# Second feed-forward stage: gate and up as seven block products of operand sums, in two passes of 544 tokens

## What is computed

```python
def swiglu(h, w_gu, w_down):
    gate, up = jnp.split(h @ w_gu, 2, axis=-1)
    return (jax.nn.silu(gate) * up) @ w_down
x = x + 0.5 * gt3 * swiglu(modulate(x, norm_ffn2, sh3, sc3), ffn2_w_gu, ffn2_w_down)
```

## Time and profile before

| | us |
|---|---|
| runs | 2447.24, 2447.64, 2450.85 |
| median of the runs | 2447.64 |
| span of the profiled execution | 2446.0 |
| PE busy in it | 2352.2 |
| DVE / POOL / ACT busy | 1107.6 / 537.6 / 386.4 |

### The profile page before, as it was taken

One profiled execution on the slowest core, in us unless ns is written; L12 is line 12 of the kernel. 1 busy time (PEld: TensorE's weight loads), 2 busy tenths in 40 slices (PEclk: granted clock), 3 DMA queues, 4 the chain that ended last, 5 costly groups with the idle time before them and its releaser, 6 DMA issues. The chain is left out here.

```text
span 2446.0 us, 50603 instructions
## 1 busy us (share of the span) xinstructions
PE 2352.2 (96%) x21666; PEld 2240.6 (92%) x21666; DVE 1107.6 (45%) x2446; ACT 386.4 (16%) x890; POOL 537.6 (22%) x278
## 2 busy tenths in 40 slices
PE   6999999999999989999888898999999999999997
PEld 5899999999999989888568885999999999999997
DVE  3634443334444365434676665147333444433344
ACT  4100000000000142434621123140000000000003
POOL 2412112212121032101331124313211212122111
PEclk8999999999999999999999999999999999999999
DMA  9232231110111042000310002332111011111102
GB/s 340 78 108 73 86 103 52 34 51 26 43 51 52 26 125 70 27 27 27 134 43 4 5 8 71 106 104 69 52 35 51 17 51 51 51 51 34 51 9 74
DMA packets 160634, 151.22 MB, mean 62 GB/s; under 512 B 21488, under 2 KB 141985, under 8 KB 160088
## 3 DMA queue, kind: packets, MB, share of 16 engines
q1 hardware_dynamic: 159960, 146.75, 19.2%
q10 hardware_dynamic: 144, 2.23, 0.2%
q0 software_dynamic: 384, 0.07, 0.0%
HBM read 137.98 MB, written 11.34 MB: 61 GB/s over the span
## 5 line engine op out<-in xcount | busy, mean ns | idle before, releaser
L487 PE MATMUL bank<-hh,f_up_hi 128*128 128x368 f32 (+1 forms) x2064 | 676.8, 328 | 1.9 <-POOL hl L412 1.0
L489 PE MATMUL bank<-hh,f_up_lo 128*128 128x368 f32 (+1 forms) x2064 | 674.7, 327 | 0.0
L488 PE MATMUL bank<-hl,f_up_hi 128*128 128x368 f32 (+1 forms) x2064 | 674.0, 327 | 0.0
L1224 DVE TENSOR_TENSOR f_prod<-f_silu,bank 128x368 f32<-128x368 f32 x132 | 70.3, 532 | 766.4 <-PE bank L489 760.1
L502 DVE SCALAR_TENSOR_TENSOR x<-bank,mods,x 128x368 f32<-128x368 f32 (+1 forms) x544 | 306.3, 573 | 200.4 <-PE bank L489 187.5
L487 PEld LDWEIGHTS bank<-hh,f_up_hi 128*128 128x128 f32 x2064 | 387.3, 188 | 7.4 <-issue 7.3
L488 PEld LDWEIGHTS bank<-hl,f_up_hi 128*128 128x128 f32 x2064 | 387.4, 188 | 0.0
L489 PEld LDWEIGHTS bank<-hh,f_up_lo 128*128 128x128 f32 x2064 | 387.4, 188 | 0.0
L955 POOL TENSOR_TENSOR f_up_lo<-f_up_raw,f_up_hi 128x2048 fp32r<-128x2048 f32 x44 | 203.3, 4621 | 776.8 <-DVE f_up_hi L1211 776.8
L487 PE MATMUL bank<-f_a_hi,f_dn_hi 128*128 128x368 f32 (+1 forms) x1056 | 346.6, 328 | 0.8 <-DVE f_scratch L505 0.8
L489 PE MATMUL bank<-f_a_hi,f_dn_lo 128*128 128x368 f32 (+1 forms) x1056 | 345.3, 327 | 0.0
(11 more groups left out here) (383 smaller groups left out, 2883.2 us busy)
## 6 DMA issues: line engine op xcount, KB each, us to landing
f_up_raw<-in_ffn_w_gu SPq DMA_DIRECT2D x88, 512.0 KB, 5.0
f_dn_raw<-in_ffn_w_down SPq DMA_DIRECT2D x22, 1024.0 KB, 7.5
ada<-in_w_ada SPq DMA_DIRECT2D x12, 1024.0 KB, 16.2
late<-in_w_ada SPq DMA_DIRECT2D x12, 1024.0 KB, 5.0
w_in_raw<-in_w_in SPq DMA_DIRECT2D x16, 512.0 KB
gates<-in_w_ada SPq DMA_DIRECT2D x8, 1024.0 KB, 5.8
x_in<-in_x_prompt SPq DMA_DIRECT2D x8, 512.0 KB, 8.5
gate<-in_w_ada SPq DMA_DIRECT2D x4, 1024.0 KB, 4.9
```

The source lines that it names most:

```text
L487: pe.matmul(out, wh, rh, start=(n == 0), stop=False)
L488: pe.matmul(out, wh, rl, start=False, stop=False)
L489: ins = pe.matmul(out, wl, rh, start=False, stop=(n == last))
L1224: dve.tensor_tensor(prod[u % 2][:, 0:n], silu[u % 2][:, 0:n], k.psum[2 * (u % 2) + 1][:, 0:n], ALU.mult).then_inc(up_free, 1)
```

## The change

The weights of a unit are seen as 2 x 2 blocks: A11 and A12 are the gate's first and second 512 input features, A21 and A22 the up's. The input of a pass is 2 x 2 as well: B11, B12 the first 512 features of its first and second tile of 272 tokens, B21, B22 the last 512. Seven products, each of 4 chunks x 3 passes, stand for the eight block products, in Winograd's form: with S1 = A22 + A21, S2 = S1 - A11, S3 = A11 - A21, S4 = A12 - S2, T1 = B12 - B11, T2 = B22 - T1, T3 = B22 - B12, T4 = B21 - T2 the products are P1 = A11 B11, P5 = S1 T1, P6 = S2 T2, P3 = S4 B22, P7 = S3 T3, P2 = A12 B21, P4 = A22 T4, in this order, and the gate and up of both tiles are sums of them. Raw weights and their low part share a place, so that a block is loaded again only after its product; units 0 and 1 of a group have one slot each. All eleven groups are run for tokens 0 to 543 (pass 0), then again for 544 to 1087 (pass 1), whose second tile has 208 prompt and the 64 sample tokens. Down takes the second tile first, in three rotating banks.

DVE now forms the sums of weights and of products and makes both parts of the hidden values (11 tensor_tensors of 272 columns and two casts a unit, and four of 512 for the weights of a next unit); the high parts of weights are ACT's (2048 and 1536 columns a unit, 2048 a group for down), the low parts POOL's as before, in the same sizes. Ahead of pass 0 the norm, the shift and four sums of 1088 columns with their high and low parts are made for both tiles at once; the norm of pass 1 is made in group 0, and its input in the last group of pass 0 (low parts on DVE, four sums on POOL). In the last group of pass 1 the four output tiles of pass 0 are turned and scaled; ten output tiles in all in place of nine. First-tile down products read `a_hi[0:272]`, the others `a_hi[272:544]`. The output projection's products stay, with the modulation's loads and products earlier in it.

```diff
-        ffn(k, "f2", dram["ffn2_w_gu"], dram["ffn2_w_down"], 6)
+        block_ffn(k, "f2", dram["ffn2_w_gu"], dram["ffn2_w_down"], 6)
...
+SH = 272
+S_TILES = [(SH * t, SH) for t in range(4)]
+KH = KD // 2
+BLK_W = KH * P
+BLK_X = KH * SH
...
+PRODUCTS = ("p1", "p5", "p6", "p3", "p7", "p2", "p4")
+W_A11, W_S1, W_S2, W_S4, W_S3, W_A12, W_A22 = range(7)
+X_B11, X_T1, X_T2, X_B22, X_T3, X_B21, X_T4 = range(7)
+PARTS = (slice(0, 4 * BLK_W), slice(4 * BLK_W, 7 * BLK_W))
...
+def block_ffn(k, name, w_gu, w_down, i_shift):
...
+    up_raw = [k.at(f"{name}_up_raw{j}", at, [P, 7 * BLK_W]) for j, at in enumerate((SLOT0_AT, SLOT1_LO_AT))]
+    up_lo = [k.at(f"{name}_up_lo{j}", at, [P, 7 * BLK_W], F32R) for j, at in enumerate((SLOT0_AT, SLOT1_LO_AT))]
...
+    prod = [k.psum[i % 4][:, 0:SH] for i in range(7)]
...
+    def down_tile(q, v):
+        return S_TILES[2 * q + 1 - v // KD]
+    def down_bank(v, last):
+        return k.psum[4 + (v % 2 if last and v >= KD else v % 3)]
...
+            def next_up(G, j, g):
+                n = of_unit(G, j) + 1
+                sp.wait_ge(prod_done[W_A11], n)
+                up_block(up_raw[j][:, w_blk(W_A11)], of_unit(g, j), 0, 0, j)
+                sp.wait_ge(up_sum, n)
+                up_block(up_tmp[j][:], of_unit(g, j), 1, 0, j)
+                sp.wait_ge(prod_done[W_A12], n)
+                up_block(up_raw[j][:, w_blk(W_A12)], of_unit(g, j), 0, 1, j)
+                sp.wait_ge(prod_done[W_A22], n)
+                up_block(up_raw[j][:, w_blk(W_A22)], of_unit(g, j), 1, 1, j)
+            def next_group(G, g):
+                next_up(G, 0, g)
+                next_up(G, 1, g)
+                sp.wait_ge(dn_mm, ND * G + ND)
+                load_dn(g)
...
+            def up_low(G, j, part):
+                pool.wait_ge(up_hi_done[part], of_unit(G, j) + 1)
+                pool.tensor_tensor(up_lo[j][:, PARTS[part]], up_raw[j][:, PARTS[part]], up_hi[j][:, PARTS[part]].bitcast(F32),
+                                   ALU.subtract).then_inc(up_lo_done[part], 1)
+            def dn_low(G):
+                pool.wait_ge(dn_hi_done, G + 1)
+                pool.tensor_tensor(dn_lo[:], dn_raw[:], dn_hi[:].bitcast(F32), ALU.subtract).then_inc(dn_lo_done, 1)
...
+            with pool.Fori(0, NGRP - 1) as g:
+                up_lows(g, 1)
+                dn_low(g)
+                up_lows(g + 1, 0)
...
+            def product(G, j, i, x_new=None):
+                f = of_unit(G, j)
+                if i in (0, 4):
+                    pe.wait_ge(up_lo_done[i // 4], f + 1)
+                if x_new is not None:
+                    pe.wait_ge(x_lo_done[i], x_new + 1)
+                if i == 0:
+                    after(pe, p7_used, f)
+                elif i == 1:
+                    after(pe, p2_used, f)
+                elif i == 2:
+                    after(pe, p4_used, f)
+                elif i == 3:
+                    after(pe, p3_used, f)
+                elif i == 4:
+                    pe.wait_ge(p1_taken, f + 1)
+                elif i == 5:
+                    pe.wait_ge(p5_taken, f + 1)
+                else:
+                    pe.wait_ge(p6_used, f + 1)
+                out = prod[i]
+                for c in range(KH):
+                    w, x = slice(BLK_W * i + P * c, BLK_W * i + P * c + P), slice(BLK_X * i + SH * c, BLK_X * i + SH * c + SH)
+                    pe.matmul(out, up_hi[j][:, w], x_hi[:, x], start=(c == 0), stop=False)
+                    pe.matmul(out, up_hi[j][:, w], x_lo[:, x], start=False, stop=False)
+                    ins = pe.matmul(out, up_lo[j][:, w], x_hi[:, x], start=False, stop=(c == KH - 1))
+                ins.then_inc(prod_done[i], 1)
+            def down(G, v, last=False):
+                a = SH * (1 - v // KD)
+                if v == 0:
+                    pe.wait_ge(dn_lo_done, G + 1)
+                    pe.wait_ge(act2_done, FC * G + FC)
+                elif v == KD:
+                    pe.wait_ge(act1_done, FC * G + FC)
+                if last and v >= KD:
+                    pe.wait_ge(dn_free, ND * G + v - 1)
+                elif v >= 3:
+                    pe.wait_ge(dn_free, ND * G + v - 2)
+                else:
+                    after(pe, dn_free, ND * G)
+                c = v % KD
+                three_passes(pe, down_bank(v, last)[:, 0:SH],
+                             [(dn_hi[:, f, P * c:P * c + P], dn_lo[:, f, P * c:P * c + P], a_hi[:, f, a:a + SH], a_lo[:, f, a:a + SH])
+                              for f in range(FC)]).then_inc(dn_mm, 1)
+            def group(G, x_new=None):
+                for j in range(FC):
+                    for i in range(7):
+                        product(G, j, i, x_new if j == 0 else None)
+                for v in range(ND):
+                    down(G, v)
...
+            def take_p1(G, j):
+                f = of_unit(G, j)
+                act.wait_ge(prod_done[0], f + 1)
+                after(act, act1_done, f - 1)
+                act.copy(p1s[j][:], prod[0]).then_inc(p1_taken, 1)
+            def take_p5(G, j):
+                f = of_unit(G, j)
+                act.wait_ge(prod_done[1], f + 1)
+                after(act, act2_done, f)
+                act.copy(p5s[:], prod[1]).then_inc(p5_taken, 1)
+            def swish(G, j, x, ready, done):
+                act.wait_ge(ready, of_unit(G, j) + 1)
+                act.activation(x[:], x[:], ACT.Silu).then_inc(done, 1)
+            def swish2(G, j):
+                swish(G, j, c12s, p3_used, silu2_done)
+            def swish1(G, j):
+                swish(G, j, p1s[j], p2_used, silu1_done)
+            def unit(G, j):
+                take_p1(G, j)
+                take_p5(G, j)
+                swish2(G, j)
+                swish1(G, j)
+            def up_high(G, j, part):
+                act.wait_ge(up_sum, of_unit(G, j) + 1)
+                act.copy(up_hi[j][:, PARTS[part]], up_raw[j][:, PARTS[part]]).then_inc(up_hi_done[part], 1)
...
+            def group(G):
+                unit(G, 0)
+                dn_high(G)
+                unit(G, 1)
+                for j in range(FC):
+                    for part in range(2):
+                        up_high(G + 1, j, part)
...
+            def up_sums(G, j, steps=range(4), tmp=None):
+                raw, a21 = up_raw[j], (up_tmp[j] if tmp is None else tmp)
+                for s in steps:
+                    if s == 0:
+                        dve.wait_ge(up_in[j], 64 * G + 64)
+                        dve.tensor_tensor(raw[:, w_blk(W_S1)], raw[:, w_blk(W_A22)], a21[:], ALU.add)
+                    elif s == 1:
+                        dve.tensor_tensor(raw[:, w_blk(W_S3)], raw[:, w_blk(W_A11)], a21[:], ALU.subtract)
+                    elif s == 2:
+                        dve.drain()
+                        dve.tensor_tensor(raw[:, w_blk(W_S2)], raw[:, w_blk(W_S1)], raw[:, w_blk(W_A11)], ALU.subtract)
+                    else:
+                        dve.drain()
+                        dve.tensor_tensor(raw[:, w_blk(W_S4)], raw[:, w_blk(W_A12)], raw[:, w_blk(W_S2)], ALU.subtract
+                                          ).then_inc(up_sum, 1)
+            def sum12(G, j):
+                n = of_unit(G, j) + 1
+                dve.wait_ge(p1_taken, n)
+                dve.wait_ge(prod_done[2], n)
+                dve.tensor_tensor(u2s[:], p1s[j][:], prod[2], ALU.add).then_inc(p6_used, 1)
+                dve.drain()
+                dve.wait_ge(p5_taken, n)
+                dve.tensor_tensor(p5s[:], u2s[:], p5s[:], ALU.add)
+                dve.drain()
+                dve.wait_ge(prod_done[3], n)
+                dve.tensor_tensor(c12s[:], p5s[:], prod[3], ALU.add).then_inc(p3_used, 1)
+            def sum22(G, j):
+                dve.wait_ge(prod_done[4], of_unit(G, j) + 1)
+                dve.tensor_tensor(p5s[:], p5s[:], prod[4], ALU.add)
+                dve.tensor_tensor(u2s[:], u2s[:], prod[4], ALU.add).then_inc(p7_used, 1)
+            def sum11(G, j):
+                n = of_unit(G, j) + 1
+                dve.wait_ge(prod_done[5], n)
+                dve.tensor_tensor(p1s[j][:], p1s[j][:], prod[5], ALU.add).then_inc(p2_used, 1)
+            def split(j, half, x, done):
+                at = slice(SH * half, SH * half + SH)
+                dve.drain()
+                dve.tensor_copy(a_hi[:, j, at], x[:])
+                dve.drain()
+                dve.tensor_tensor(a_lo[:, j, at], x[:], a_hi[:, j, at].bitcast(F32), ALU.subtract).then_inc(done, 1)
+            def second(G, j):
+                dve.drain()
+                dve.wait_ge(silu2_done, of_unit(G, j) + 1)
+                dve.tensor_tensor(c12s[:], c12s[:], p5s[:], ALU.mult)
+                split(j, 1, c12s, act2_done)
+            def first(G, j):
+                dve.wait_ge(prod_done[6], of_unit(G, j) + 1)
+                dve.tensor_tensor(u2s[:], u2s[:], prod[6], ALU.add).then_inc(p4_used, 1)
+                dve.drain()
```

(20 more changed lines are left out.)

616 lines of the change are left out of this document (579 added, 37 removed).

## The result

The changed kernel takes 2676.55 us (median of 4 runs, 2671.77 to 2682.86) where the kernel before takes 2449.24 in the same comparison (2447.24 to 2451.66): ratio 1.0932, 95% interval 1.0912 to 1.0952. It is 9.3% slower. Predicted were 2667 us. The profiled execution has a span of 2670.0 us against 2446.0.

A forecast was written before the change was run, and what follows sets the result against it. Matmuls bound the second feed-forward stage before; POOL holding DVE would after. 71.6 + 40 + 8 x 41.3 + 59 + 55.6 + 9 x 46.5 + 49 + 9 = 1033 us replaced 813, giving 2667 us, range 2510 to 2740.

The forecast's parts named there:

- PE's saving: Second feed-forward stage: matmul work falls from 779 to 697 us at 120 ns each, 82 us less, 53 to 117 by bounds.
- The exclusive work: DVE casts and two-SBUF operations wait while POOL subtracts; 11.1 us of DVE plus 20.9 of POOL make 32.0 a group.
- The group of 41.3 us: Pass 0 group: 31.7 us of PE plus 9.6 of waits at product seven, before down and for down banks.
- the one of 46.5: Pass 1 group: 31.7 us of PE plus 2.8, 1.8, 5.4, 3.0 and 1.8 make 46.5 us.
- The second pass: Pass 1: the samples' 64-column adds wait for POOL, PE waits 5.4 and 3.0 us, then runs at DVE's pace.
- rival B: TensorE's clock falls after pass 1's waits: 3 us a group in 10 to 21 groups, 2697 to 2730 us; chance 0.15.
- Start, switch, end: Stage edges: first group ends 71.6 us after the projection, groups around the switch 59 and 55.6, last 49, tail 9.
- A: DVE slips between POOL's instructions: groups of 32.7 and 34.9 us, whole 2429 us, 2417 to 2442; chance 0.16.
- C: The second collision in a group falls between POOL's subtracts once: 4 to 6 us less a group, 2550 to 2590; chance 0.17.
- D: Matmuls of 272 columns cost 135 ns or more, so PE saves nothing; the forecast total stays; chance 0.02.

The follow-up runs named there:

- the series: Kernel before with series of 144 fp32r matmuls at widths of 256 to 512 columns added behind its end: 126.1 ns start to start at 272 columns.
- short_psum: Changed kernel with the samples' gated sum through PSUM in the second pass and POOL's weight subtractions in pieces of 256 columns: 2533.12 us, ratio 1.0347.

## Why the prediction was right

**PE's saving: too large.** The prediction took 120 ns a matmul between bounds of 114 and 125. The kernel shows 126.0 in the products and 125.6 in down, and the series confirm it. So PE's work fell from 779 to 5808 x 0.126 = 732 us, 47 us less where 82 were written, just outside both bounds (125 ns, 53 us). The lower bound was carried on from a step of 8.8 ns for 16 columns; 352 and 368 happen to stand 1 ns apart from the line that all widths make, and a slope from two neighbours carried that over 80 columns. As the prediction said, the total doesn't hang on it, since the chain left PE.

**The exclusive work: right in kind, and in where it bites.** Casts and operations with both operands in SBUF stand until POOL is through, PSUM readers don't: 1010 against 220 ns for the same add is the proof, and a cast took 0.68 us for 0.30 in short_psum's row. The group of 41.3 us measured 41.0, the one of 46.5 measured 46.4, and in the first pass the steps are the ones foretold. By the timelines of its nine groups, POOL's down subtraction runs mostly from 14.4 to 19.1 us after the group's start (13.5 to 18.2 written). A 256 KB load landed after 2.9 us, not 3.8, so one weight sum gets in before it and the second is held; the fourth ends at 21.1 (21.0 written), and product seven starts at 21.5, as written. TensorE's waits come in the four places named but are shorter: 1.8 us at product seven (2.8 written), 1.75 before down (1.8), 1.05 and 2.25 beside the next unit's low parts (1.5 and 2.9). Its matmuls take 33.3 of the group where 31.7 were written. The two errors cancel, and not by luck: DVE and POOL set the moments at which TensorE may go on, and a slower TensorE arrives at them later and waits less, as the prediction said of its bounds. What the prediction put in as a reason, that 32.0 us of exclusive work nearly fills PE's 31.7, was the weaker half of it: pieces raised the sum and gave time back. The schedule of holds was what counted, and that is how the 41.3 was worked out.

**The second pass: right in kind, the number with some luck.** 5.3 us of the 5.4 by which it is longer than the first came back by the operand's place (46.4 to 41.1 on average). In its groups the long waits are 4.3 and 2.0 us where 5.4 and 3.0 were written, and with those ahead of them 9.7 in all where 13.0 were. The rest of a group beside waits and 33.3 us of matmuls is 3.4 us where 1.8 were written, and part of this is the lower clock, which the 46.5 left to rival B.

**Start, switch, end.** The projection's last matmul ended at 1635.6 in the profiled execution (1633.5 before: 2 us come from ahead of the stage). The first product began 5.9 us later and the first group ended 72.3 us later; 5.5 and 71.6 were predicted. The switch took 58.2 and 53.1 against 59 and 55.6. In the last group the final down product ended at 2655.1, 49.9 us after the group's start, against 49; the tail behind it took 14.9 against 9, the one term here that was off, where before's had 12. The stage is 1034.4 us, 1033 predicted. The weight loads, written as 5 MB a group, are 3 (77 GB/s over 41 us); nothing waited for them.

**Rivals.** A (no collisions, 2429) did not come. Its condition, nearly no loss to blocking, was produced by hand, and even then the time was 2476, not 2429. Its groups were 32.7 and 34.9 and measured 33.6 and 35.3, 12 us over the 18 groups and mostly the 126 ns; start and switch were written as 52 and 77 and measured 62 and 86; last group and tail 57.5 and 64.8; the rest lay ahead of the stage in that execution. So the chance of 0.13 for faster looks too high: it rested on a PE saving of 82 us, and with the measured 47 no run of the changed kernel, POOL's work left out or not, came under the kernel before.

B came in part: the clock was at its lower level for 162 of the 1028 us from the first product on, and for 85 of the 417 us in the nine groups of the second pass. There it falls during the long wait of a group, about 31 us after the group's start, and that is not free. The groups that start at 2234.4 and 2280.2 run alike to 0.02 us up to the end of their last long wait. From there the clock stays low for 3.1 us in the one and for 5.1 in the other. The 6.2 us from that wait on in each:

```profile
core 0: us, PE busy (x), PEclk, DMA share, GB/s
2270.20:2276.40 6.20, 6.20 (x38) 0.75 0.00 0
2316.00:2322.20 6.20, 6.20 (x31) 0.59 0.00 0
```

38 matmuls against 31 with TensorE busy throughout, and the groups take 45.8 and 46.5 us. The other groups lean the same way, less sharply: 45.7 and 46.4 at a granted clock of 0.93, 46.5 to 47.2 at 0.89; the one at 0.85 takes 46.0, and its added lower stretch lies ahead of the long wait. No run shows such a group at full clock. As an estimate, six matmuls took 1.36 us there, 227 ns each where 126 is the full clock's, so 3.1 and 5.1 us can have cost 1.4 and 2.3 us at most. B had the mechanism and its price at 3 us; the forecast had none of it.

C did not come. D is out, with 126 ns.

## What to carry over

A smaller operation count is bought with DVE and POOL work; price each such operation by where its operands lie, and draw up one period of the loop with POOL's instructions in it, since a hold costs only where TensorE waits for what is held. If both must run, give DVE an operand in PSUM, put its SBUF sums where nobody waits, and cut POOL's instructions shorter, and look for the length anew (256 columns was the best of the four tried here; at 128 one add no longer got in, and once it did, POOL itself was late). But first ask whether the change could win without any collision: here 47 us of matmuls saved stood against 69 us more beside them, above all at the starts of two passes.

## What was new of the hardware

- A row of POOL instructions of 128 columns that follow each other at 0.42 us held one DVE add for 9.41 us, though a DVE sum of another line got in beside such a row after one piece (0.97 us for 0.69). At 256 columns and 0.69 us, no DVE operation beside such pieces in the ordinary groups took over 1.28 us. A drain of POOL behind every second piece let the add in (mean 5.0 to 0.63 us). Between 128 and 256 columns nothing was tried, and what decides at 128 is open.
- A matmul of fp32r with its weight load costs columns / 2.4 plus 12 to 14 ns from 256 to 384 columns and at 512, and 20 at 448; the latter has no explanation here.
- A wait costs more than its own length. The clock fell in TensorE's waits of 4.3 us and stayed low for some us of work behind them: 31 matmuls in 6.2 us where the neighbouring group, with its clock back 2 us sooner, did 38.
